# Twelve modulation chunks of a layered trunk step moved ahead of the first attention, with shorter DVE chains and copies on ACT

## What is computed

```python
m = (jax.nn.silu(c) @ w_mod + b_mod).reshape(c.shape[0], 6, 1, D_MODEL)   # shift, scale, gate, twice
...
yp = yp + mp[2] * o_p                                                    # o_p: attention or SGU
yp = yp + mp[5] * peer(modulate(rms_norm(yp, norm2_g[i]), mp[3], mp[4]), *pw)
...
t1, i1 = lax.top_k(s1, PEER_TOPK)                                        # peer: 8 heads, 16 of 128 keys, twice
cand = (t1[..., :, None] + t2[..., None, :])...
top, ci = lax.top_k(cand, PEER_TOPK)
idx = e1 * N_KEYS + e2
act = jax.nn.gelu(jnp.einsum('thkd,td->thk', u_tab[idx], xt))
return jnp.einsum('thk,thkd->td', g * act, v_tab[idx])
```

## Time and profile before

| | us |
|---|---|
| median of 3 runs | 2215.53 |
| lowest and highest | 2204.23, 2223.11 |
| span of the profiled execution | 2207.0 |

### The profile page before, as it was taken

How to read it: one execution, slowest core, us unless ns; L and a number is a source line. 1 busy time by engine, 2 the same in 40 slices (tenths; PEclk the granted TensorE clock), 3 DMA queues, 4 the chain that set the end, 5 groups by cost and what they waited for, 6 DMA issues and landing times. The chain is left out here.

```text
span 2207.0 us, 25764 instructions
## 1 busy us (share of the span) xinstructions
PE 1531.2 (69%) x9198; PEld 745.6 (34%) x9198; DVE 1395.3 (63%) x3469; ACT 355.5 (16%) x901; POOL 1212.1 (55%) x1097
## 2 busy tenths in 40 slices
PE   5676446865546879977687889968778850555567
PEld 2345113541123426533532437525423310111112
DVE  1447988599875655558498836499687327443641
ACT  0100112111112211013131201122223110111111
POOL 0004377545777574437475754467675438745774
PEclk8687778987877979888796888977887785578658
DMA  9719899998989899898798998989998889999998
GB/s 366 276 47 403 291 374 335 413 362 329 384 323 370 297 417 419 341 364 315 274 347 316 315 362 345 377 324 338 363 339 302 323 317 338 380 419 419 335 350 310
DMA packets 213942, 751.57 MB, mean 341 GB/s; under 512 B 27236, under 2 KB 35628, under 8 KB 213816
## 3 DMA queue, kind: packets, MB, share of 16 engines
q0 software_dynamic: 155136, 564.20, 68.4%
q1 hardware_dynamic: 58680, 185.72, 21.6%
HBM read 747.74 MB, written 2.10 MB: 340 GB/s over the span
## 5 line engine op out<-in xcount | busy, mean ns | idle before, releaser
L779 POOL DMA_INDIRECT uring<-in_peer_u,expert x512 | 580.6, 1134 | 511.5 <-DVE dots L1932 211.0
L1217 PE MATMUL yacc<-vring,diag 64*64 64x512 f32 x4096 | 653.6, 738 | 229.9 <-DMA vring<-in_peer_v,expert 163.2
L779 POOL DMA_INDIRECT vring<-in_peer_v,expert x512 | 556.4, 1087 | 425.8 <-PE yacc L1217 290.4
L1932 DVE CUSTOM_DVE_ANT_0 uring<-uring,h 128x1024 f32<-128x1024 f32 x512 | 615.3, 1225 | 161.4 <-DMA uring<-in_peer_u,expert 144.1
L1217 PEld LDWEIGHTS yacc<-vring,diag 64*64 64x64 f32 x4096 | 155.2, 156 | 610.0 <-DMA vring<-in_peer_v,expert 338.8
L1453 ACT ACTIVATE diag<-cst,wts 128x64 f32<-128x64 f32 (+1 forms) x528 | 172.9, 344 | 868.7 <-PE yacc L1217 630.0
L1005 PE MATMUL pp<-hT,wring 128*128 128x128 f32 x992 | 132.3, 294 | 21.7 <-issue 15.9
L1005 PEld LDWEIGHTS pp<-hT,wring 128*128 128x128 f32 x992 | 125.8, 208 | 35.4 <-issue 29.6
L1805 DVE TENSOR_REDUCE arena<-arena 128x16 f32<-128x1024 f32 x64 | 77.8, 1215 | 28.6 <-ACT arena L1392 27.7
L1706 DVE MAX8 t<-sc 128x8 f32<-128x128 f32 (+1 forms) x68 | 19.9, 292 | 117.5 <-ACT sc L1253 83.2
L1068 PE MATMUL pq<-w_uk,arena 128*128 128x512 f32 x128 | 74.6, 672 | 22.9 <-ACT arena L1392 22.9
(11 more groups left out here) (301 smaller groups left out, 1854.0 us busy)
## 6 DMA issues: line engine op xcount, KB each, us to landing
wring<-in_peer_w_q SPq DMA_DIRECT2D x47, 1024.0 KB
wring<-in_w_mod SPq DMA_DIRECT2D x38, 1024.0 KB
wring<-in_sg_w_in SPq DMA_DIRECT2D x48, 768.0 KB
wring<-in_sg_w_out SPq DMA_DIRECT2D x18, 1024.0 KB
wring<-in_mla_w_o SPq DMA_DIRECT2D x9, 1024.0 KB
uring<-in_peer_u,expert POOLq DMA_INDIRECT x512
vring<-in_peer_v,expert POOLq DMA_INDIRECT x512
uring<-in_w_mod SPq DMA_DIRECT2D x6, 1024.0 KB, 16.7
```

What stands on the lines that cost most here:

```text
L779: pool.indirect_dma_start(ring[:, slot % RING, :], None, table[n // 3], bass.IndirectOffsetOnAxis(ap=idx, axis=0)).then_inc(land[slot % RI ...
L1217: last = pe.matmul(yacc[64 * q:64 * q + 64, r], diag[at, slot % RING, :], v[at, 512 * q:512 * q + 512], start=first, stop=final)
L1932: dve.tensor_tensor_reduce(u, u, rows_h[:, :], 1.0, 0.0, ALU.mult, ALU.add, dots[:, p % 2, i:i + 1]).then_inc(u_used, 1)
```

## The change

1. The 12 `mod` chunks between the routes of tile A become entries of `EARLY`: the three points of `mla_in` get 4, 4 and 8 chunks, those of `attn` stay 4, 4 and 0. 32 chunks are now used before the output projection.
2. The sum of squares of a prompt tile's norm, the copy of the gate row out of PSUM (`proj`, `sgu_out`, `peer_out`) and `drain` go from DVE to ACT.
3. `rsqrt` has three links in an iteration in place of four, `polynomial` two in place of three. `pick` treats both halves in one set of operations of 512 columns.
4. All five tables of order are new.

```diff
-189:VVVVVVVVVVVVVVVV 197:VVV 199:V 200:VVVVV 207:V 208:VVVVVV 213:VVV 217:VV 218:V 232:V 237:VV 239:V 260:VV 280:V
+158:VVVVV 161:VV 165:VVVVVVVVV 173:VV 174:V 176:V 177:VVVVV 179:VVV 184:V 185:VVV 190:VVV 193:VV 194:VV 210:VV 217:V
...
     caches = [("cache", b) for b in range(NT)]
-    era0 = (woven(first[2:], mods(0, 20, 24) + mods(1, 0, MODS_EARLY)) +
+    era0 = (first[2:] +
             [("norm", B, 0, 0), ("mla_in", B), ("attn", B), ("proj", B), ("norm", B, 0, 1)] + woven(heads(1, (4, 4)), mods(1, MODS_EARLY, 12)) +
...
 EARLY = {}
-_early = mods(0, 8, 20)
-for _s, _n in ((("norm", A, 0, 0), (0, 0)), (("mla_in", A), (0, 2, 2)), (("attn", A), (4, 4, 0))):
+_early = mods(0, 8, 24) + mods(1, 0, MODS_EARLY)
+for _s, _n in ((("norm", A, 0, 0), (0, 0)), (("mla_in", A), (4, 4, 8)), (("attn", A), (4, 4, 0))):
     for _j, _m in enumerate(_n):
...
             return ["ssq", "hT0", "hT1"] + rep, ["sq", "h"], ["hT0", "hT1"] + rep
-        return ["rows", "hT0", "hT1"], ["h"], ["hT0", "hT1"]
+        return ["rows", "hT0", "hT1"], ["h"], ["sq", "hT0", "hT1"]
     if kind == "mla_in":
...
     if kind == "proj":
-        return ["row"] * (tile != S) + ["w0", "w1", "w2", "w3"], ["row"] * (tile != S) + ["x"], []
+        return ["row"] * (tile != S) + ["w0", "w1", "w2", "w3"], ["x"], ["row"] * (tile != S)
     if kind == "query":
...
     if kind == "sgu_out":
-        return ["row"] * (tile != S) + [f"w{i}" for i in range(6)], ["row"] * (tile != S) + ["x"], []
+        return ["row"] * (tile != S) + [f"w{i}" for i in range(6)], ["x"], ["row"] * (tile != S)
     if kind == "peer_out":
-        return ([], ["x"], []) if tile % 3 == S else (["y"], ["x"], [])
+        return ([], ["x"], []) if tile % 3 == S else (["y"], ["x"], ["row"])
     return [], [], []
...
         sc, work = sb("sc", [P, 4, 2, NKEYS]), sb("work", [P, 256])
-        t1, ti = sb("t1", [P, 2, TOPK]), sb("ti", [P, 2, TOPK], U32)
-        cand, hot = sb("cand", [P, TOPK * TOPK]), sb("hot", [P, TOPK, TOPK])
-        ctop, ci, cu = sb("ctop", [P, TOPK]), sb("ci", [P, TOPK], U32), sb("cu", [P, 2, TOPK], U32)
+        t1, picks = sb("t1", [P, 2, TOPK]), sb("picks", [P, 4, TOPK], U32)
+        cu, ti = picks[:, 0:2, :], picks[:, 2:4, :]
+        hot = sb("hot", [P, 2, TOPK, TOPK])
+        cand = hot[:, 0].rearrange("p a b -> p (a b)")
+        ctop, ci = sb("ctop", [P, TOPK]), sb("ci", [P, TOPK], U32)
         cf, ef = sb("cf", [P, 4, TOPK]), sb("ef", [P, 2, TOPK])
...
             return yacc[:, row % 2] if row < rows_before(FIRST_QUERY) else pq[:, 1]
+
+        def last_slot(n):
+
+            return SLOT0[max(p for p, s in enumerate(STEPS) if s[0] == n) + 1]
...
                 begin(act, k)
+                if tile != S:
+                    if k == WHERE[("norm", A, 0, 0)]:
+                        act.wait_ge(in_x, 16)
+                    signal(act.activation(h_tok[tile][:, :], x[tile][:, :], ACT.Square, accum_out=scr[:, 0:1]), "sq")
                 for q in range(2):
...
+            def gate_row(k, tile, name):
+
+                after(act, PE, k, name)
+                signal(copy(h_tok[tile][:, :], pss[:, :, :].rearrange("p q n -> p (q n)")), "row")
+
+            def projection(k, tile):
+                begin(act, k)
+                if tile != S:
+                    gate_row(k, tile, "row")
+                for j in range(n_points(k) - 1):
+                    point(k, j)
+
+            def peer_out(k, n):
+                if n % 3 != S:
+                    begin(act, k)
+                    gate_row(k, n % 3, "y")
+
             def query(k, n, h, g):
...
-            spot = Spots(PLAN_ACT, D=diagonal, T=tanh)
+            def drain(i):
+
+                n = DRAINED[i]
+                act.wait_ge(v_used, last_slot(n))
+                copy(h_tok[n % 3][:, :], yacc[:, :, :].rearrange("p q n -> p (q n)")).then_inc(drained, 1)
+
+            spot = Spots(PLAN_ACT, D=diagonal, T=tanh, Y=drain)
...
                           cache=cache, sgu_v=sgu_v, sgu_vnorm=sgu_vnorm, sgu_u=sgu_u, sgu_mix=sgu_vnorm,
-                          sgu_s=sgu_s, sgu_s_mix=sgu_s_mix)
+                          sgu_s=sgu_s, sgu_s_mix=sgu_s_mix, proj=projection, sgu_out=projection, peer_out=peer_out)
...
                 signals.end()
-            assert spot.done == dict(D=N_SLOTS, T=len(STEPS))
+            assert spot.done == dict(D=N_SLOTS, T=len(STEPS), Y=len(DRAINED))
...
                     link(tt(tmp, out, out, ALU.mult))
-                    link(tt(tmp, tmp, v, ALU.mult))
-                    link(ts(tmp, tmp, -0.5, 1.5, ALU.mult, ALU.add))
-                    link(tt(out, out, tmp, ALU.mult))
+                    link(stt(tmp, tmp, -0.5, v, ALU.mult, ALU.mult))
+                    link(stt(out, tmp, 1.5, out, ALU.add, ALU.mult))
...
                 else:
-                    square_sum(scr[:, 0:1], xr, h)
+                    after(dve, ACTE, k, "sq")
                 link(ts(scr[:, 0:1], ps[0][:, 0:1] if tile == S else scr[:, 0:1], 1.0 / D, EPS, ALU.mult, ALU.add))
...
                 else:
-                    if SCHEDULE[k][0] == "peer_out":
-                        link(cp(h, flat(pss)))
+                    after(dve, ACTE, k, "row")
                     link(tt(h, h, flat(acc), ALU.mult))
...
-            def gate_row(k, tile):
-
-                if tile != S:
-                    after(dve, PE, k, "row")
-                    signal(cp(h_tok[tile][:, :], flat(pss)), "row")
-
             def proj(k, tile):
                 begin(dve, k)
-                gate_row(k, tile)
                 for i in range(4):
...
                 begin(dve, k)
-                gate_row(k, tile)
                 for i in range(6):
...
                 link(ts(cu[0:r, 1, :], ci[0:r, :], 15, None, ALU.bitwise_and))
-                link(cp(cf[0:r, 0:2, :], cu[0:r, :, :]))
-                link(cp(cf[0:r, 2:4, :], ti[0:r, :, :]))
-                for i in range(2):
-                    hr = hot[0:r, :, :]
-                    link(tt(hr, over(cf[0:r, i, :], TOPK), times(const("iota16", r), TOPK), ALU.is_equal))
-                    link(tt(hr, hr, times(cf[0:r, 2 + i, :], TOPK), ALU.mult))
-                    link(dve.tensor_reduce(ef[0:r, i, :], hr, X, ALU.add))
+                link(cp(cf[0:r, :, :], picks[0:r, :, :]))
+                hr, h3 = hot[0:r, :, :, :], hot[0:r, :, :, :].rearrange("p i a b -> p (i a) b")
+                link(tt(h3, over(cf[0:r, 0:2, :].rearrange("p i a -> p (i a)"), TOPK), times(const("iota16", r), 2 * TOPK),
+                        ALU.is_equal))
+                link(tt(hr, hr, cf[0:r, 2:4, :].unsqueeze(2).to_broadcast([r, 2, TOPK, TOPK]), ALU.mult))
+                link(dve.tensor_reduce(ef[0:r, :, :].rearrange("p i a -> p (i a)"), h3, X, ALU.add))
                 link(stt(expert_out, ef[0:r, 0, :], float(NKEYS), ef[0:r, 1, :], ALU.mult, ALU.add))
...
-                then(tt(out, a, a, ALU.mult))
-                then(ts(out, out, GELU_C, 1.0, ALU.mult, ALU.add))
-                return tt(out, out, a, ALU.mult)
+                then(stt(out, a, GELU_C, a, ALU.mult, ALU.mult))
+                return stt(out, out, 1.0, a, ALU.add, ALU.mult)
...
-            def last_slot(n):
-                return SLOT0[max(p for p, s in enumerate(STEPS) if s[0] == n) + 1]
-
-            def drain(i):
-
-                n = DRAINED[i]
-                dve.wait_ge(v_used, last_slot(n))
-                cp(h_tok[n % 3][:, :], flat(yacc)).then_inc(drained, 1)
-
...
-            spot = Spots(PLAN_DVE, U=dot, P=gelu, W=weights, Y=drain)
+            spot = Spots(PLAN_DVE, U=dot, P=gelu, W=weights)
...
                 signals.end()
-            assert spot.done == dict(U=N_SLOTS, P=len(STEPS), W=len(STEPS), Y=len(DRAINED))
+            assert spot.done == dict(U=N_SLOTS, P=len(STEPS), W=len(STEPS))
...
```

More of the change, by code:

```diff
@@ new lines @@
+145:DDT 149:DD 162:D 165:DTD 172:D 176:DDDDDD 178:D 180:DDD 181:D 186:D 190:D 192:D 194:D 197:DDDDD 198:D 199:DDD
+205:D 207:DT 208:DD 210:DD 215:DDDDDD 216:D 218:D 222:D 224:D 226:D 227:DDDTDDD 231:DDDDDDDDDDDDD 232:T 244:DD 245:T
+249:DDD 253:D 262:DDDDDDDD 270:D 271:D 273:TD 274:D 275:D 277:Y 280:DDDD 284:DDDDDD 289:DD 291:D 292:D
+294:DDDDTDDDDDDD 299:DDD 318:D 319:D 322:TD 328:D 340:DD 342:DD 343:D 345:D 346:DD 349:D 350:DDD 362:DD 370:D 372:DT
+374:D 379:DD 384:D 386:D 387:D 389:DDDDDDDDDDD 394:T 395:D 399:D 400:DD 402:D 403:DD 406:D 408:DDDD 411:DD 413:D
@@ L136 @@
+704:TDDDDDDDDDDTD 708:DD 709:TDDDDDDD 711:D 712:DDD 717:D 719:D 720:D 729:D 737:DD 739:T 740:D 742:DDD 745:D
+753:DDDDDDDDDDDD 767:DDT 770:DDDDD 776:DDDDDDD 778:DDDDDD 783:DDDTDDD 784:DDDDDDDDDDDTDDDDDDDDDTDDDDDDDDDDDDD
+786:DDDDDY 787:DD 788:DDDD
 """
 PLAN_DVE = """
[L138 to L140 removed]
@@ L172 @@
-516:WWWWWWWWWW
+4:WW 7:WWWWWW 13:WWW 14:WWW 22:W 24:W 26:WW 31:WWW 35:WWWWWWWWWWWWWWWWW 47:WWWWWWWWW 53:WWWWWWWWWW 56:W 58:WWWWWWWWWW
+65:W 82:W 91:WWW 101:WWWW 107:W 114:W 117:W 142:W 188:WWWWWWWWWWWWW 196:WWWWWWWWW 198:WWWW 201:WWW 207:WWWW
```

(2 more changed lines are left out.)

98 lines of the change are left out of this document (47 added, 51 removed).

## The result

The changed kernel took 2241.45 us (median; 2234.89 to 2242.33), the kernel before 2214.1 us beside it: ratio 1.0131, 95% interval 1.0093 to 1.0170. The forecast was 2180 us, faster. The profiled execution's span is 2233.1 us, against 2207.0.

The account below looks back on a forecast made before the run. The DMA was taken to bound the kernel as a whole, DVE between 163 and 284 us. Terms 2 - 9 - 9 - 3 - 6 - 3 - 5 - 3 = -36 took 2207.0 to 2171, on the median 2180 us; range 2160 to 2200.

Parts of the forecast that it names:

- The new tables at nothing: Whole kernel: new tables of order cost nothing, since dot and value-sum counts at norms, routes and residuals stay nearly equal.
- Work on ACT at nothing, hidden where ACT waits anyway: Squares, gate rows and drains: 25 us off DVE, hidden on ACT, which is busy 16%; nothing taken for the path.
- A missed sign: Whole span, among the signs that would show the forecast right: ACT busy near 375 us.
- The opening, +2: Up to the first gather: 2 us longer, first gather at about 165 us, bounds -3 and +8.
- Step (a): Opening: constant loads stand behind seven more chunks in SP's queue, so DVE's first work on z is 4.6 us late.
- (b): Opening, PE's chunks up to attention: last of 32 lands at 101 to 103 us; first softmax 2 us later, second 3.
- the bound of +8: Opening's slow bound: 8 us longer if everything from 50 us on moves at 380 instead of 420 GB/s.
- The DVE edits: Route, rsqrt, polynomial and moves to ACT: together 81 us less DVE work, counting only where DVE binds.
- 163 to 284 us, -9: Eight first routes, where DVE binds: 9 us gained from DVE work, the ten departing chunks' 25 us mostly not gained.
- 284 to 600 us, -9: Next stretch: 12 to 13 us less DVE work, DMA with 22 us of room; 9 us gained, between 5 and 13.
- The gather queue rival: Behind the first gather: POOL's new gather order blocks and DMA share falls; at 0.90, 2244 us; chance 0.10.
- rule of 21.6 us for each 0.01: Behind the first gather: each 0.01 of DMA share below 0.93 costs 21.6 us; slower than before from 0.91 on.

Follow-up runs that it names:

- E14: Changed kernel with all the work moved to ACT back on DVE, new order kept: 1.0220 of the kernel before, 2132.5 us.
- E16: Kernel before with short DVE chains and moved chunks, all else on DVE, order of before: 0.9929 of the kernel before, 2073.5 us.
- E10: Changed kernel with all work back on DVE, drains too, new order kept: 1.0141 of the kernel before.
- E8: Kernel before with short DVE chains and moved chunks, nothing on ACT, order of before: 0.9938 of the kernel before.
- E6: Kernel before with only squares, gate rows and drains on ACT, 66 diagonals moved just behind such places: 1.0151 of the kernel before.
- E3: All code of the change in the order of before, except 66 diagonals placed behind the work on ACT: 1.0102 of the kernel before.
- E17: Same kernel as E3, measured in another group: 1.0112 of the kernel before.
- E13: The changed kernel itself, measured again in another group: 1.0194 of the kernel before.
- E5: Kernel before with only the twelve chunks moved ahead of attention, all else in the order of before: 1.0007 of the kernel before.
- E2: Changed kernel with the twelve constant loads issued behind eight chunks again, not behind eighteen: 1.008 of the kernel before.
- E4: Kernel before with only the shorter DVE chains (rsqrt, polynomial, picks), whole order as before: 2190.5 us, 0.9899 of the kernel before.
- E18: E16 with only POOL's gather sequence taken from the new order: 1.0295 of the kernel before.
- E19: E16 with PE, ACT and DVE in the new order, POOL and SP in that of before: 1.0523 of the kernel before.
- E1: Changed kernel with eight squares and eight gate rows back on DVE, the four drains still on ACT: 1.0018 of the kernel before.

## Why the prediction was wrong

**The new tables at nothing: this step failed.** I compared how many dots and value sums stand ahead of each norm and route, found them nearly equal, and costed the rest, the fine grain, at nothing. The tables cost 2.9% between E14 and E16 in one group (2.0% if E10 is set against E8, across two groups). The count was also given too widely: it holds at the first four norms, but 457 dots stand ahead of the square sum of the sample tile's norm of layer 1 before and 463 after, the place of the largest single loss, and 416 and 451 ahead of tile A's last residual. The other losses don't show in such counts. What counts is whether a dot stands between a residual and its norm, and, as I read PE's waits, whether a diagonal is issued before its value sum is due; the second was not tested by itself.

**Work on ACT at nothing, hidden where ACT waits anyway: this step failed too.** ACT is busy 16%, but what it issues next often stands in a wait for a value sum, and everything behind waits with it. In E16, with the order of before:

```profile
ACT diag L1455 <- PE yacc L1219: 741.9, 391, 24.6
```

As long as only diagonals stood behind such a wait, nothing else was held up by it. Cost: 1.5% in E6, 1.6% between E3 and E8, 1.8% between E17 and E16. The Trainium skill, "Perfetto Trace Analysis", section "Optimizing Scalar/DVE Operations", says that offloading some work to Scalar may make sense when DVE is saturated. Here DVE's relief was real (1346.8 us busy in E14, 1322.5 in E13) and the runs deny the gain. Part of this cost may lie with the 66 diagonals that I placed behind; the squares' rows show 38 us of it in five norms. In the new order the work on ACT costs nothing measurable (E13 against E14). The two costs do not add: from residual to norm result the same five norms took 66 us in E16, 82 in E14 and 87 in E13: the new order pays 16 us by itself and 5 for the squares, where the order of before paid 38 for them. ACT's wait above fell to 411.5 us in E14. I read the new order as one made to keep ACT free, and PE's longer waits for diagonals as its price; that reading is argued, the numbers are shown. Tables and work on ACT together make the changed kernel 2.7% slower than E16 in the same group (1.0194 and 0.9929). A missed sign belongs here: ACT stood at 353.5 us busy where I forecast 375. The 20 us are there in E6 (379.3, against 359.5 in E5), but the new order alone takes 23 off.

**The opening, +2: mis-sized, +10.3 us.** Step (a) said 4.6 us late at z; it was 8.9 (62.76 against 53.88). E2 took it away and the first gather hardly moved, so the term that decides is (b): the last of the 32 chunks was to land by 101 to 103 us and the second softmax to come 3 us late. The second reciprocal on DVE, which stands behind that chunk's row, before:

```profile
101.98 0.17 DVE L1654 RECIPROCAL scr<-scr 128x4 f32<-128x4 f32 x1
```

and in the changed kernel, with PE's wait for the last chunk:

```profile
110.80 1.07 PE L881 MATMUL yacc<-uring,siluT 128*32 128x256 f32 x16 [0.65 <-DMA uring<-in_w_mod]
112.79 0.17 DVE L1693 RECIPROCAL scr<-scr 128x4 f32<-128x4 f32 x1
```

The chunk landed at 110.8 us and the reciprocal came 10.8 us late, as much as the whole opening. From 50 to 110.8 us the DMA was full (share 0.99) but moved 373 GB/s, where the step took 420 and kept 380 for the bound of +8. In E2 it moved 410 GB/s and the last chunk still landed only at 107.1 us, so the bytes were counted 1 to 2 MB short, too.

**The DVE edits: right in size, wrong in place.** DVE's busy time was forecast at 1314 us and measured at 1322.6; the 81 us hold about 10 us of gaps, which are no busy time (and 34 routes at 0.81 us make 27.5, not 26). E4 gained 22 us. **163 to 284 us, -9, and 284 to 600 us, -9:** the sum was right (-18 up to the sample norm), the division wrong: -16 and -2 by the table. That the sum fits is luck in good part, since both terms were credited to DVE and the chunks at nothing. With the chunks in place the short chains gained nothing between the first gather and tile B's norm (122.35 us before, 123.8 in E4). With the chunks gone it took 109.2 us in E5 against 116.6 in E6 of the same group (which has the work on ACT, too). Only then do the short chains count: 103.3 us in E8. The stretches of E5 and E8 (columns as in the earlier trace rows):

```profile
173.75:282.96 109.21, 51.77 (x352) 35.28 (x351) 101.29 (x339) 11.11 (x36) 50.10 (x48) 0.73 0.74 266
175.23:278.49 103.26, 48.42 (x344) 34.43 (x347) 96.19 (x307) 11.12 (x36) 48.62 (x46) 0.75 0.76 275
```

With 0.034 us for each instruction DVE's time is 113 and 107 us, no less than the stretches, and the DMA stands at 0.74 and 0.76. So DVE binds here once the ten chunks are out, and not before: 112.9 of 120.65 us was near the bound and not at it. That the relief is not gained in all was right, but because the opening takes it back.

**The gather queue rival** (0.10) described the symptom: share 0.91, from which its rule of 21.6 us for each 0.01 gives 2050 us behind the first gather, and it was 2059. POOL's wait for value sums grew from 290.7 us to 321.5. But between E14 and E16, where the 2.9% lie, it did not grow (261.3 and 262.2 us), so that growth is not where the loss sits. The rival's cause, POOL's sequence by itself, is not shown either: E18 costs 3.7% against E16 (across two groups), E19, without that sequence, more still; the sequence and its consumers must fit.

**Left open.** E1 (1.0018) differs from E10 and E14 (1.014, 1.022) only in who does the drains; I can't tell the drains' share from the difference between groups or from E1's spread. What SP's new order does by itself, and the losses between the single places named, were not tested.

## What to carry to other kernels

Compare two orders by what stands between the links of the critical chain, instruction by instruction; counts at stage boundaries miss most of it, and a count at four of them says nothing of the others. An order has a price, here 2 to 3% with the same instructions and bytes. An engine that is 16% busy but mostly standing in waits isn't free: a moved instruction inherits the waits ahead of it in the queue. Bring in parts of a change one by one: the short chains alone made the kernel 1% faster. Two parts can also need each other: here the short chains gained nothing behind the first gather until the chunks were out.
